# A mixer's tail buffers moved to dead scratch, and one expert load moved ahead of the stage that uses it

## The reference, cut to what matters

```python
def token_mixer(...):
    ...
    y = sigmoid(parts[11]) * (y_a @ w_pa) + sigmoid(parts[12]) * (y_b @ w_pb)   # merge
    return y @ w_out                                                            # output projection

x = x + g1 * mix_lat
h2 = rms_norm(x, norm2_g) * (1.0 + sc2) + sh2
x = x + g2 * hier_moe_2(h2, w_group, b_group, w_router, b_router, w_gate, w_up, w_down)
return rms_norm(x, final_norm_g)

def hier_moe_2(h, ...):
    ...                                    # logits, best group, two best experts, weights
    for e in range(32):
        a = silu(tok @ w_gate[e]) * (tok @ w_up[e])
        out = out + combine[:, e:e + 1] * (a @ w_down[e])
```

## Time and profile before

| | before |
|---|---|
| median of 3 runs | 1572.54 us (1571.43, 1572.54, 1575.5) |
| span of the profiled execution | 1574.9 us |
| PE busy | 1353.3 us (86% of the span) |
| DVE busy | 689.2 us (44%) |
| ACT busy | 247.8 us (16%) |
| POOL busy | 80.0 us (5%) |
| moved by DMA | 528.20 MB, mean 335 GB/s |

### The profile page before, as it was taken

How to read it: one execution, slowest core, us unless ns; L and a number is a source line. 1 busy time by engine, 2 the same in 40 slices (tenths; PEclk the granted TensorE clock), 3 DMA queues, 4 the chain that set the end, 5 groups by cost and what they waited for, 6 DMA issues and landing times. The chain is left out here.

```text
span 1574.9 us, 27743 instructions
## 1 busy us (share of the span) xinstructions
PE 1353.3 (86%) x11912; PEld 876.2 (56%) x11912; DVE 689.2 (44%) x1844; ACT 247.8 (16%) x505; POOL 80.0 (5%) x125
## 2 busy tenths in 40 slices
PE   9999998997978789899999999999896676666665
PEld 8655554553455566588767748886453343333332
DVE  4634664322223343427687536652562332332333
ACT  2322330110001111233223113230200000000000
POOL 2401000000000000030000200100000000000000
PEclk9999999999988999999999999999998878887887
DMA  9965899999999999877522454476999999999996
GB/s 336 270 232 191 335 426 429 424 425 427 427 430 425 426 425 427 352 251 280 200 93 106 148 174 160 165 284 257 381 393 429 429 430 429 431 430 430 430 427 252
DMA packets 94023, 528.20 MB, mean 335 GB/s; under 512 B 8282, under 2 KB 10610, under 8 KB 67684
## 3 DMA queue, kind: packets, MB, share of 16 engines
q1 hardware_dynamic: 88792, 521.30, 81.8%
q0 software_dynamic: 2624, 5.32, 1.4%
q10 hardware_dynamic: 2508, 0.17, 0.1%
HBM read 525.70 MB, written 1.07 MB: 334 GB/s over the span
## 5 line engine op out<-in xcount | busy, mean ns | idle before, releaser
L1568 PE MATMUL ps<-weight_ring,e_xT 128*32 128x256 f32 x3456 | 247.8, 449 | 131.4 <-DMA weight_ring<-in_w_up_dram 89.2
L1568 PEld LDWEIGHTS ps<-weight_ring,e_xT 128*32 128x32 f32 x3456 | 137.0, 128 | 237.6 <-issue 192.7
L1848 DVE TENSOR_TENSOR e_g<-e_act_g,ps 128x128 f32<-128x128 f32 x64 | 24.8, 388 | 263.5 <-ACT e_act_g L1655 262.3
L1846 DVE TENSOR_TENSOR e_act_g<-e_act_g,ps 128x128 f32<-128x128 f32 x32 | 9.2, 286 | 236.2 <-ACT e_act_g L1655 236.2
L1655 ACT ACTIVATE e_act_g<-ps 128x128 f32<-128x128 f32 x64 | 17.8, 278 | 565.5 <-PE ps L1568 558.3
L1568 PE MATMUL ps<-expert_set,e_xT 128*32 128x256 f32 x640 | 51.3, 491 | 42.5 <-DMA expert_set<-in_w_up_dram 42.5
L1598 PE MATMUL ps<-weight_ring,e_gT 128*32 128x256 f32 x1344 | 82.6, 387 | 4.2 <-DVE e_gT L1852 2.0
L2369 PE MATMUL ps<-expert_set,weight_ring 128*128 128x256 f32 x384 | 84.2, 379 | 0.0
L2369 PEld LDWEIGHTS ps<-expert_set,weight_ring 128*128 128x128 f32 x384 | 73.0, 190 | 9.9
L1532 PE MATMUL ps<-e_y,e_routing 32*128 32x256 f32 x1024 | 74.3, 404 | 2.1 <-DVE e_y L1880 1.5
L1524 PE MATMUL ps<-e_n,e_Gt 128*32 128x256 f32 x1056 | 70.9, 385 | 3.8 <-DVE e_Gt L1795 2.0
(11 more groups left out here) (614 smaller groups left out, 1945.4 us busy)
## 6 DMA issues: line engine op xcount, KB each, us to landing
weight_ring<-in_expert_w_dram SPq DMA_DIRECT2D x80, 2048.0 KB, 23.0
weight_ring<-in_w_in_dram SPq DMA_DIRECT2D x26, 2048.0 KB, 9.6
weight_ring<-in_w_down_dram SPq DMA_DIRECT2D x20, 2048.0 KB, 38.8
weight_ring<-in_w_gate_dram SPq DMA_DIRECT2D x19, 2048.0 KB, 32.9
weight_ring<-in_w_up_dram SPq DMA_DIRECT2D x19, 2048.0 KB, 37.4
weight_ring<-in_w_ada_dram SPq DMA_DIRECT2D x12, 2048.0 KB, 12.6
expert_set<-in_w_gate_dram SPq DMA_DIRECT2D x10, 2048.0 KB, 33.4
expert_set<-in_w_up_dram SPq DMA_DIRECT2D x10, 2048.0 KB, 37.9
```

What stands on the lines that cost most here:

```text
L1568: mm = pe.matmul(ps[32 * j:32 * j + 32, 4, 0:256].rearrange("p (w f) -> p w f", w=2), xT[:, k, :], w13[:, :, k, j * P:(j + 1) * P], start= ...
L1848: dve.tensor_tensor(g[:], spread(act_g[:]), spread(ps[:, 4, P:2 * P]), ALU.mult).then_inc(s_g, 1)
```

## The change

Three things change. `hT` moves from `nT`'s place to that of `yT`, which the output projection has read by then, and `spare` from `nTp`'s place to the stretch of FT where `junk` was; `junk` becomes four smaller pieces of other scratch. That leaves slot 2 of `c.three` unused from filler 15 on, and SP loads the third down there behind piece 22, in the second mixer, and no longer at the beginning of the second experts. ACT waits once more, ahead of its third square, since one piece of `junk` now lies on the row buffer of the modulation, which must have been written out (`s_arow`).

```diff
-            for i in (2, 4) if last else (3,):
+            for i in (4,) if last else (3,):
                 load_down(i)
...
-        hT, spare = nT, nTp[:].rearrange("p k n -> p (k n)")
+        hT, spare = yT, FT[:, 4128:4128 + 2048]
...
-        junk = FT[:, 4128:4128 + 2048]
+        junk = [misc[:, 512 * g:512 * g + 512] for g in range(3)] + [FT[:, 2080:2592]]
...
+            W = [t[x] for x in ("w_gate_2", "w_up_2", "w_down_2")]
             for p in M2_ISSUE:
                 sp.wait_ge(*used(M2_BEFORE[p]))
                 m2_load(c, sp, t, p)
-            W = [t[x] for x in ("w_gate_2", "w_up_2", "w_down_2")]
+                if p == 22:
+                    sp.wait_ge(s_fl, 16)
+                    load_one(c, sp, c.s_e2, 2, 2, W, third=c.three)
...
-                act.activation(junk[:, g * 512:g * 512 + 512], h[:, tile, half * 512:half * 512 + 512], ACT.Square,
+                act.activation(junk[g], h[:, tile, half * 512:half * 512 + 512], ACT.Square,
                                accum_out=stat[:, 0, at:at + 1]).then_inc(s_hsq, 1)
...
                 act.wait_ge(s_h, g + 1)
+                if g == 2:
+                    act.wait_ge(s_arow, 48)
                 squares(g)
```

## The result

| | before | after |
|---|---|---|
| median of 9 runs each, us | 1575.5 (1571.43 to 1576.65) | 1578.39 (1576.0 to 1583.18) |
| ratio, 95% interval | | 1.0025 (1.0014 to 1.0036) |
| span of the profiled execution, us | 1574.9 | 1574.3 |
| PE busy, us | 1353.3 | 1347.5 |

What follows compares the result with a forecast made beforehand. The second expert stage was taken as bound by DMA bytes, its stream's start by PE freeing a buffer. Terms 0 + 1.6 + 0 + 0 = +1.6 us on the three-run median 1572.54 gave 1574.1 us, range 1569.2 to 1577.5.

Steps and rivals of the forecast that it cites:

- what bounds the end: Second expert stage: DMA bytes at 429 GB/s; its stream starts at the 1148.70 us issue, waiting for a buffer PE frees.
- the freed load is worth nothing: Second expert stage's begin: removing the third down's 2.10 MB load gains 0, bounds 0 and 4.9 us.
- The rival by which the freed transfer counts: Stream from 1124 us on is one piece: 1569.2 us with the delay (chance 0.10), 1567.6 without (0.04).
- the chain of the delay: Second mixer's tail: piece 33 4.89 us later, less DVE's idle 0.99 and PE's slack 2.33, delays PE's transposes 1.57 us.
- The rival of a hidden delay: Last modulation piece arrives under 3.3 us later, so nothing changes: 1572.5 us; chance 0.20.
- The 4.89 us for the transfer: SP's queue behind piece 22: the third down's 2.10 MB at 429 GB/s delays the last modulation piece by 4.89 us.
- the size of the idle time: PE ahead of its transposes at 1055.47 us: idle 1.57 us, giving the forecast's +1.6 us.
- the moved buffers: nothing: Buffers lie elsewhere with the same operations, and ACT's added wait has 45.8 us of room: cost 0.
- The upper bound of 3.2 us: Upper bound on PE's delay: 6.5 us, by the spacing of two downs, less 3.32 us of slack.
- The third rival: PE's idle time at 1055.5 us lowers its clock, losing 3.4 us besides the 1.6 delay: 1577.5 us; chance 0.07.
- The time from 1148.70 on: From the issue of the pair of loads behind the second expert to the end: the same 426 us as before.
- The range's upper end of 1577.5: Whole kernel: the range's slow end, set at the clock's case of 1.6 + 3.4 = 5.0 us.

Runs made afterwards that it cites:

- the dose: Changed kernel with half, then three quarters, of the third down loaded behind piece 22, the rest behind piece 33; single times 1573.84 and 1578.08 us.
- one kernel without idle time: Changed kernel with the third down loaded behind piece 33 instead of ahead of it; 1575.22 us against 1575.23 before, ratio 0.9998.

## Why the prediction was right and wrong, step by step

**Right: what bounds the end, and that the freed load is worth nothing.** Read from the earlier trace rows as an issue that waits for PE, it was borne out twice: by 0.9998 for the same saving without the delay, and by the 4.6 us between the medians that most of a like load costs once the stream runs. The rival by which the freed transfer counts was wrong.

**Right: the chain of the delay.** Piece 33, DVE's sums, the covers of 0.99 and 2.33 us, PE's idle time and the issue of the gate followed in the order and with the slack forecast; the dose shows the slack to 0.1 us. The rival of a hidden delay was wrong. The 4.89 us for the transfer measured 4.82. By the Trainium skill, "DMA: Bandwidth & Descriptors", section Bandwidth, the prediction had an estimate of 5.86 us from 358 GB/s, which that section gives as a core's part where both cores of a pair stream. The dose's 435 GB/s, measured with the kernel on one core, does not agree with that figure, and that its shift of 2.5 us was nearer to the 2.9 is luck.

**Wrong: the size of the idle time, 1.57 us for a measured 2.90.** The step that failed is "the moved buffers: nothing". With them alone piece 33 came 1.43 us later than in the one profile of before. Alone this is hidden under 3.32 us of slack, as the kernel with the moved buffers shows. But the load had already used up that slack in full: 4.82 + 1.43 = 6.25, 6.32 by DVE's row, and less 3.32 that is 3.0. I had looked for the cost of the buffers where they are used, in ACT's order, and not at the other end of the delay that I had just priced. What in them delays the piece stays open; the instruction packet is the likely way. The upper bound of 3.2 us, taken from the spacing of two loads, held the value, by luck, since it was a bound on the transfer. Luck, too, is that the pair behind the second expert goes out 1.67 us later, counted from piece 22, as if the forecast's 1.6 had held: it is 2.96 us less the 1.29 of column B.

**Wrong: the clock's chance.** The third rival had 0.07, against it the 1.75 us of idle time at 164 us with the clock at 1.00. That row holds no single gap of this length: by PE's timeline of before it is one of 0.53 and one of 1.23 us. What it was taken to say was right for the size forecast: at 0.52 and 1.59 us of idle time, one execution each, the clock stayed. At 2.9 us it fell in three of four executions. The row was read as evidence on an idle time of 1.57 us, and fell with that number. The price was put at 3.4 us; where the clock fell it was 1.3 to 4.5. The Trainium skill, "TensorE: Matmul & The Clock Gate", section "HAM oscillation — how this bites in real kernels", says that a wait for a DMA between blocks of matmuls makes the next block start cold. I had put it aside for an idle time of the size forecast. These three executions agree with it and the fourth does not, and the waits of its example are longer than this one.

**Not foreseen: what came back.** The time from 1148.70 on was to stay at 426 us; in the four executions it was 424.2 to 424.5, since the last expert ran at the full clock (column C).

**The baseline.** Of the 4.3 us between the forecast of 1574.1 and the measured 1578.39, 3.0 are the baseline's: the forecast stood on a median of three runs that was 3.0 us under the median of nine. The other 1.3 are the change's, +2.9 instead of +1.6. That +2.9 between the medians is not simply the idle time's 2.90: in the profiles the clock behind it adds 1.8 and 2.9 come back later. The range's upper end of 1577.5 left the three runs' spread of 4 us out around the likeliest case, taking it as covered by the other cases, and lay too low by 0.9 us. As a share of the time the change is 0.25%, inside the 0.3% that the prediction called the limit of a measurement; with nine and eleven runs and the kernel before beside them the intervals were narrower than that.

## What to carry to other kernels

A slack can be spent once: add up all delays that reach the same wait, those of edits that look free among them, before the slack is subtracted, and take a chance of the clock's loss behind the idle time that is left into the sum. A load moved to where the DMA engines look idle is worth its bytes only if the stream behind it starts earlier; ask which instruction issues that stream's first load, and whom it waits for. And a load put ahead of a piece that an engine already waits for is paid in full, where one place further back it is free.

## What the runs showed of the hardware

A transfer of 2.10 MB over 16 engines ended 1.1 to 1.45 us late on one share alone, next to a 16 KB packet of an instruction queue that takes 1.1 us; an edit that moved no load, some buffers and a wait of ACT, came with such a delay of 1.43 us. Idle times of PE of 0.5 and 1.6 us ahead of the transposes left the granted clock at 1.00, 2.8 to 2.9 us brought it to 0.50 in three executions of four, for 1.3 to 4.5 us of loss. And the later falls of the clock differ between executions: 1.3 us in the routing and some 2 us at the last expert came back in every execution of the changed kernel. That PE's shift moves them is not shown: one kernel without idle time took 13.27 us for the routing in two executions and 12.00 in the third, and its stretch D was 552.2, 551.7 and 550.0 us.
